# One decoder-layer step on one core: the front of an mLSTM + pooling + MoE kernel rearranged in six places

## The reference

```python
x1 = LN1(alpha*x + W_out [pool_group(x) | mlstm_group(x)])
x2 = LN2(alpha*x1 + MoE(x1))            # top 4 of 32 experts, clamped SwiGLU
y  = x2 + sigmoid(x2 W_pg) * (p W_ple)
```

```python
def mlstm_chunk(carry, inp):
    C, n, m = carry
    ...
    m_t = jnp.maximum(inter, jnp.max(logD, axis=-1))
    Dw = jnp.exp(logD - m_t[..., None]); sc = jnp.exp(inter - m_t)
    qk  = jnp.einsum('bhtk,bhsk->bhts', q, k) * Dw
    num = jnp.einsum('bhts,bhsv->bhtv', qk, v) + sc * (C q)
    den = jnp.sum(qk, axis=-1) + sc * (n q)
    ...
    C_new = decay * C + jnp.einsum('bhsv,bhsk->bhvk', v * wk, k)
    n_new = decay * n + jnp.einsum('bhs,bhsk->bhk', wk, k)
```

## Time and profile before

| | us |
|---|---|
| median of 3 runs (lowest, highest) | 1123.28 (1123.21, 1123.94) |
| span of the profiled execution, first to last instruction | 1122.0 |
| median of the runs less that span (the profiled execution has no other time of its own) | 1.3 |
| PE busy | 1102.2 (98%) |
| DVE / ACT / POOL busy | 410.8 / 165.4 / 78.3 |
| DMA moved | 440.45 MB, mean 393 GB/s |

### The profile page before, as it was taken

How to read it: one execution, slowest core, us unless ns; L and a number is a source line. 1 busy time by engine, 2 the same in 40 slices (tenths; PEclk the granted TensorE clock), 3 DMA queues, 4 the chain that set the end, 5 groups by cost and what they waited for, 6 DMA issues and landing times.

```text
span 1122.0 us, 14800 instructions
## 1 busy us (share of the span) xinstructions
PE 1102.2 (98%) x5706; PEld 428.6 (38%) x5706; DVE 410.8 (37%) x875; ACT 165.4 (15%) x310; POOL 78.3 (7%) x102
## 2 busy tenths in 40 slices
PE   8999999999999999999999999999999999999998
PEld 6788433333333333333333333333333333323344
DVE  1657583333333333333333333333333333222255
ACT  1423141001000100010001100010001000100033
POOL 0756610000000000000000000000000000000000
PEclk9999999999999999999999999999999999999999
...
GB/s 318 261 341 240 253 286 403 427 428 428 429 428 429 429 427 429 427 429 428 430 428 428 429 427 429 429 429 428 428 429 428 429 429 429 427 429 427 428 280 39
DMA packets 47699, 440.45 MB, mean 393 GB/s; under 512 B 10512, under 2 KB 11788, under 8 KB 22741
## 3 DMA queue, kind: packets, MB, share of 16 engines
...
q10 hardware_dynamic: 292, 0.56, 0.1%
...
## 4 chain that ended last, share of the span: by engine, by line
PE 87%; DMA 10%; DVE 2%; ACT 0%; issue 0%; SPq 0%; DVEq 0%; ACTq 0%
PE bank L883 36%; PE bank L925 18%; DMA ring<-in_w_mlp 9%; PE bank L822 7%; PE bank L510 6%; PE bank L844 5%; PE bank L1001 2%; PE bank L686 2%; PE bank L857 2%; PE bank L907 2%; PE bank L870 1%; PE bank L914 1%; PE bank L850 1%; DMA ring<-in_w_in 1%; PE bank L836 1%
## 5 line engine op out<-in xcount | busy, mean ns | idle before, releaser
L883 PE MATMUL bank<-ring,proj 128*64 128x512 f32 x2048 | 466.0, 597 | 4.7 <-DMA ring<-in_w_mlp 4.7
L1395 DVE SCALAR_TENSOR_TENSOR xT<-bank,proj,xT 128x512 f32<-128x512 f32 x128 | 90.2, 747 | 440.9 <-PE bank L844 439.5
L883 PEld LDWEIGHTS bank<-ring,proj 128*64 128x64 f32 x2048 | 135.3, 136 | 288.7 <-issue 246.9
L925 PE MATMUL bank<-ring,wpool 128*64 128x512 f32 x1024 | 225.1, 592 | 0.0
L925 PEld LDWEIGHTS bank<-ring,wpool 128*64 128x64 f32 x1024 | 71.2, 136 | 130.0 <-issue 129.2
L1744 ACT ACTIVATE proj<-proj 128x256 f32<-128x256 f32 x64 | 26.7, 417 | 546.7 <-DVE proj L1424 546.7
L822 PE MATMUL bank<-xreg,proj 128*64 128x512 f32 (+1 forms) x396 | 95.4, 599 | 0.1
L510 PE MATMUL bank<-xT,ring 128*128 128x264 f32 x320 | 76.3, 396 | 2.9 <-DVE proj L1058 2.4
L844 PE MATMUL bank<-mixT 64*128 64x512 f32 x264 | 74.5, 641 | 0.5 <-ACT mixT L1752 0.5
L510 PEld LDWEIGHTS bank<-xT,ring 128*128 128x128 f32 x320 | 61.4, 195 | 15.6 <-DVE proj L1058 2.8
L1752 ACT COPY mixT<-bank 128x512 f32<-128x512 f32 x32 | 18.8, 586 | 232.4 <-PE bank L925 232.4
...
## 6 DMA issues: line engine op xcount, KB each, us to landing
...
```

Of the source, the lines that this page charges most:

```text
L883: last = pe.matmul(bank[q][BLOCK * t:BLOCK * (t + 1), :], xgT[:, k % 4, k // 4, :], ring[:, s, col:col + 512], start=False, stop=(k == KD ...
L925: last = pe.matmul(bank[4][BLOCK * h:BLOCK * (h + 1), :], aT[:, m, BLOCK * t:BLOCK * (t + 1)], w[:, k % 2, 512 * h:512 * h + 512], start=F ...
L1395: ins = STT(total[:, c, s], ins_bank[h][:, :], gate_table[:, c, bass.ds(n, 1)], total[:, c, s], ALU.mult, ALU.add)
```

## The change

It has six parts. (1) `vtok`, `vweighted` and `CT` get a 129th column per head (`WIDE`), which is 1 in `vtok`; the six groups of one-column products per head (L535, L544, L663) go, and a product's result is 129 columns, heads 0 to 2 in one bank and head 3 in bank 3. (2) The maxima diagonal of chunk 1 stands on partitions 32 to 35 instead of 0 to 3. (3) DVE copies tile 4 out between the two chunks' rows instead of behind both. (4) The first 512 columns of `w_in` are loaded as two halves of 256 columns with all rows (1 KB runs instead of 2 KB), and the other constants are issued by SP between them instead of by ACT at the start. (5) POOL clears a tile `blank`, and PE multiplies it with itself four times, 256 columns each, before it waits for the identity. (6) The transpose of `scq` is moved ahead of the second `mix`.

```diff
-xreg = sb("xreg", [P, 3 * D])
-lnreg = sb("lnreg", [P, 2 * D])
+xreg = sb("xreg", [P, 3 * D + 8])
+lnreg = sb("lnreg", [P, 2 * D + 8])
+blank = mixT[:, :, :].rearrange("p k n -> p (k n)")[:, 1024:1024 + 2 * P]
...
+def wide(main, at, lo, hi):
+    if hi <= 3:
+        return main[:, 0:3 * WIDE].rearrange("p (h d) -> p h d", h=3)[:, lo:hi]
+    return bank[3][:, at:at + WIDE].unsqueeze(1)
+V0, M0, V1 = 0, WIDE, 2 * WIDE
+I1, M1 = V0, M0
+HEAD_SETS = ((0, 3), (3, 4))
...
-xtok = xreg[:, :].rearrange("p (c d) -> p c d", c=3)
+xtok = xreg[:, 0:3 * D].rearrange("p (c d) -> p c d", c=3)
-vtok = xreg[:, 1024:2048].rearrange("p (c h d) -> p c h d", c=2, h=HEADS)
-decayed = xreg[:, 2048:3072].rearrange("p (c h t) -> p c h t", c=2, h=HEADS)
+vtok = xreg[:, 1024:2056].rearrange("p (c h d) -> p c h d", c=2, h=HEADS)
+decayed = xreg[:, 2056:3080].rearrange("p (c h t) -> p c h t", c=2, h=HEADS)
-vweighted = lnreg[:, 1024:1536].rearrange("p (h d) -> p h d", h=HEADS)
-CT = lnreg[:, 1536:2048].rearrange("p (h d) -> p h d", h=HEADS)
+vweighted = lnreg[:, 1024:1540].rearrange("p (h d) -> p h d", h=HEADS)
+CT = lnreg[:, 1540:2056].rearrange("p (h d) -> p h d", h=HEADS)
...
-maxdiag = [xreg[0:HEADS, 2048 + 512 * c:2560 + 512 * c].rearrange("p (h t) -> p h t", h=HEADS)
+maxdiag = [xreg[32 * c:32 * c + HEADS, 2056 + 512 * c:2568 + 512 * c].rearrange("p (h t) -> p h t", h=HEADS)
...
-    for c, (t0, n) in enumerate(CHUNKS):
+    for c in (0, 1, 2):
+        t0, n = CHUNKS[c]
+    def load_columns(half):
+        sp.dma_start(ring[:, half, :].rearrange("p (k n) -> p k n", k=KD),
+                     w_in[0, :, 256 * half:256 * half + 256].rearrange("(k p) n -> p k n", p=P))\
+          .then_inc(sem(f"slot{half}"), 16)
...
-    load_block(0)
+    load_columns(0)
+    sp.dma_start(cst[:, C_ID + P:C_END], consts[:, C_ID + P:C_END]).then_inc(sem("cst_in"), 16)
+    load_columns(1)
...
+    pe.wait_ge(sem("pool_chain"), 2)
+    for _ in range(4):
+        pe.matmul(bank[7][:, 0:2 * P], blank[:, 0:P], blank, start=True, stop=True)
...
-            s = 2 * b + k // 4
-            if j == 0 and k % 4 == 0:
-                pe.wait_ge(sem(f"slot{s}"), 16)
-            w = ring[:, s, :].rearrange("p (k n) -> p k n", k=4)
-            last = pe.matmul(bank[t % 2][:, 0:TOK], w[:, k % 4, j * P:(j + 1) * P], xT[:, k, :],
-                             start=(k == 0), stop=(k == KD - 1))
+            if b == 0:
+                if j % 2 == 0 and k == 0:
+                    pe.wait_ge(sem(f"slot{j // 2}"), 16)
+                w = ring[:, j // 2, :].rearrange("p (k n) -> p k n", k=KD)[:, k, (j % 2) * P:(j % 2 + 1) * P]
+            else:
+                s = 2 * b + k // 4
+                if j == 0 and k % 4 == 0:
+                    pe.wait_ge(sem(f"slot{s}"), 16)
+                w = ring[:, s, :].rearrange("p (k n) -> p k n", k=4)[:, k % 4, j * P:(j + 1) * P]
+            last = pe.matmul(bank[t % 2][:, 0:TOK], w, xT[:, k, :], start=(k == 0), stop=(k == KD - 1))
...
         pe.matmul(bank[7][:, 0:TOK], wpool[:, g, :], proj[:, T_U + g, :], start=True, stop=True)\
           .then_inc(sem("pool_ps"), 1)
-    def values(c, dst, dden):
+    def values(c, dst, at):
         for h in range(HEADS):
-            pe.matmul(dst[:, h * P:(h + 1) * P], decayed[:, c, h, :], vtok[:, c, h, :], start=True, stop=True)
+            last = pe.matmul(wide(dst, at, *HEAD_SETS[h // 3])[:, h % 3, :], decayed[:, c, h, :], vtok[:, c, h, :],
+                             start=True, stop=True)
+        return last
+    def memory(c, dst, at):
         for h in range(HEADS):
-            last = pe.matmul(dden[:, h:h + 1], decayed[:, c, h, :], ones[:, 0:1], start=True, stop=True)
-        return last
-    def memory(c, dst, dn):
-        for h in range(HEADS):
-            pe.matmul(dst[:, h * P:(h + 1) * P], ktok[:, c, h, :], vweighted[:, h, :], start=True, stop=True)
-        for h in range(HEADS):
-            w0 = 4 * (ROW_WK + c) + h
-            last = pe.matmul(dn[:, h:h + 1], ktok[:, c, h, :], gcol[:, w0:w0 + 1], start=True, stop=True)
+            last = pe.matmul(wide(dst, at, *HEAD_SETS[h // 3])[:, h % 3, :], ktok[:, c, h, :], vweighted[:, h, :],
+                             start=True, stop=True)
         return last
     def turn_heads(c):
...
-    values(0, bank[2], bank[3][:, 0:4]).then_inc(sem("num_ps"), 1)
+    values(0, bank[2], V0).then_inc(sem("num_ps"), 1)
-    memory(0, bank[4], bank[3][:, 4:8]).then_inc(sem("mem_ps"), 1)
+    memory(0, bank[4], M0).then_inc(sem("mem_ps"), 1)
...
-    values(1, bank[5], bank[3][:, 8:12])
+    values(1, bank[5], V1)
-        pe.matmul(bank[2][:, h * P:(h + 1) * P], proj[:, T_Q + h, P:2 * P], CT[:, h, :], start=True, stop=True)
-    for h in range(HEADS):
-        last = pe.matmul(bank[3][:, 12 + h:13 + h], proj[:, T_Q + h, P:2 * P], nstate[:, h:h + 1],
+        last = pe.matmul(wide(bank[2], I1, *HEAD_SETS[h // 3])[:, h % 3, :], proj[:, T_Q + h, P:2 * P], CT[:, h, :],
-    memory(1, bank[4], bank[3][:, 16:20]).then_inc(sem("mem_ps"), 1)
+    memory(1, bank[4], M1).then_inc(sem("mem_ps"), 1)
...
     mix(0, first, range(4))
     pe.wait_ge(sem("sbc_done"), 2)
     turn_heads(0)
-    pe.wait_ge(sem("num_done"), 2)
-    mix(1, second, range(4))
     pe.wait_ge(sem("cfin_done"), 1)
     pe.wait_ge(sem("scq_ready"), 1)
     pe.transpose(bank[7][0:STATES, 0:P], scq, ident).then_inc(sem("scq_ps"), 1)
+    pe.wait_ge(sem("num_done"), 2)
+    mix(1, second, range(4))
     pe.wait_ge(sem("hT_done"), 1)
     mix(0, first, range(4, KD))
     turn_heads(1)
     pe.wait_ge(sem("ct_ready"), 2)
     for h in range(HEADS):
-        pe.transpose(bank[4][:, h * P:(h + 1) * P], CT[:, h, :], ident)
-    pe.transpose(bank[3][0:HEADS, 0:P], nstate, ident).then_inc(sem("cfin_ps"), 1)
+        pe.transpose(bank[4][:, h * P:(h + 1) * P], CT[:, h, 0:HD], ident)
+    pe.transpose(bank[3][0:HEADS, 0:P], CT[:, :, HD], ident).then_inc(sem("cfin_ps"), 1)
     pe.wait_ge(sem("sample_heads"), 2)
     pe.transpose(bank[7][:, P:P + STATES], srow[:, SY, :], ident[0:STATES, 0:STATES])\
...
-    empty_tile(4)
+        if c == 0:
+            empty_tile(4)
...
-    step(dve.tensor_copy(vtok[:, 0], bank[2][:, :].rearrange("p (h d) -> p h d", h=HEADS)))
+    more(dve.memset(vtok[:, :, :, HD:WIDE], 1.0))
+    step(dve.tensor_copy(vtok[:, 0, :, 0:HD], bank[2][:, :].rearrange("p (h d) -> p h d", h=HEADS)))
-            .to_broadcast([P, HEADS, P]), ALU.mult), "vw_ready")
+            .to_broadcast([P, HEADS, WIDE]), ALU.mult), "vw_ready")
-    step(dve.tensor_copy(nstate, bank[3][:, 4:8]))
-    step(dve.tensor_copy(den, bank[3][:, 0:4]))
-    step(dve.tensor_copy(CT, bank[4][:, :].rearrange("p (h d) -> p h d", h=HEADS)), "ct_ready")
-    step(dve.tensor_copy(hout[:, 0], bank[2][:, :].rearrange("p (h t) -> p h t", h=HEADS)), "num_done")
+    for lo, hi in HEAD_SETS:
+        more(dve.tensor_copy(CT[:, lo:hi, :], wide(bank[4], M0, lo, hi)))
+        more(dve.tensor_copy(hout[:, 0, lo:hi], wide(bank[2], V0, lo, hi)[:, :, 0:HD]))
+        more(dve.tensor_copy(den[:, lo:hi], wide(bank[2], V0, lo, hi)[:, :, HD]))
+    dve.wait_ge(sem("dve_chain"), counts["dve_chain"])
+    dve.engine_nop().then_inc(sem("num_done"), 1)
+    more(dve.engine_nop(), "ct_ready")
-            .to_broadcast([P, HEADS, P]), ALU.mult), "vw_ready")
+            .to_broadcast([P, HEADS, WIDE]), ALU.mult), "vw_ready")
...
-    step(TT(hout[:, 1], bank[2][:, :].rearrange("p (h t) -> p h t", h=HEADS),
-            sc1.unsqueeze(2).to_broadcast([P, HEADS, P]), ALU.mult))
-    step(TT(hout[:, 1], hout[:, 1], bank[5][:, :].rearrange("p (h t) -> p h t", h=HEADS), ALU.add))
-    step(TT(den, bank[3][:, 12:16], sc1, ALU.mult))
-    step(TT(den, den, bank[3][:, 8:12], ALU.add), "num_done")
+    for lo, hi in HEAD_SETS:
+        inter = wide(bank[2], I1, lo, hi)
+        more(TT(hout[:, 1, lo:hi], inter[:, :, 0:HD],
+                sc1[:, lo:hi].unsqueeze(2).to_broadcast([P, hi - lo, P]), ALU.mult))
+        more(TT(den[:, lo:hi], inter[:, :, HD], sc1[:, lo:hi], ALU.mult))
+    dve.wait_ge(sem("dve_chain"), counts["dve_chain"])
+    for lo, hi in HEAD_SETS:
+        inner = wide(bank[5], V1, lo, hi)
+        more(TT(hout[:, 1, lo:hi], hout[:, 1, lo:hi], inner[:, :, 0:HD], ALU.add))
+        more(TT(den[:, lo:hi], den[:, lo:hi], inner[:, :, HD], ALU.add))
+    dve.wait_ge(sem("dve_chain"), counts["dve_chain"])
+    dve.engine_nop().then_inc(sem("num_done"), 1)
-    step(TT(CT, CT, dec_b.unsqueeze(2).to_broadcast([P, HEADS, P]), ALU.mult))
-    step(TT(CT, CT, bank[4][:, :].rearrange("p (h d) -> p h d", h=HEADS), ALU.add))
-    step(TT(nstate, nstate, dec_b, ALU.mult))
-    step(TT(nstate, nstate, bank[3][:, 16:20], ALU.add), "ct_ready")
+    step(TT(CT, CT, dec_b.unsqueeze(2).to_broadcast([P, HEADS, WIDE]), ALU.mult))
+    for lo, hi in HEAD_SETS:
+        more(TT(CT[:, lo:hi, :], CT[:, lo:hi, :], wide(bank[4], M1, lo, hi), ALU.add))
+    dve.wait_ge(sem("dve_chain"), counts["dve_chain"])
```

(5 more changed lines are left out.)

4 lines of the change are left out of this document (2 added, 2 removed).

## The result

| | us |
|---|---|
| median of the changed kernel, 4 runs (lowest, highest) | 1113.53 (1113.17, 1115.05) |
| the kernel before on the same chip, 4 runs (lowest, highest) | 1123.61 (1123.21, 1124.52) |
| ratio | 0.9908, 95% interval 0.9896 to 0.9920 |
| profiled execution of the changed kernel: time, span | 1113.78, 1112.0 |

The change gains 10.1 us; the sum had 8.25. What happened is nearest to rival (B): PE asked for more than the forecast, and a new wait for DVE took a part of it back. In many executions, whichever the kernel, the granted clock falls for some 3.5 us somewhere in the front, which makes that execution 1.6 to 1.7 us longer (rows at the end); the two profiles compared here have no such stretch.

The account below looks back on a forecast made before the run. The weight stream was taken to bound the end, its start set by PE's way through the front. Gains 0.75 + 0.4 + 2.3 + 0.9 + 1.55 + 2.35 = 8.25 us gave 1115.0, from 1123.28; range 1113.3 to 1118.2.

Parts of the forecast that it names:

- rival (B): Front: clock stays high from the dummies on, q rows' chain makes PE wait for `vweighted`; gain 9.0 to 9.4, 1114.1; chance 0.10.
- first product: Front start: slot 0 lands near 9.2 and the first product starts at 9.6 instead of 10.36; gain 0.75, ends 0 and 1.0.
- What bounds the kernel: Expert loop: the weight stream sets the end, so PE reaching the loop X us earlier moves the end by X.
- (C): Loop start: early pair loads come too late, so the end does not follow; 3 to 4 us gained, 1119.5; chance 0.09.
- (D): Expert loop: tiles shifted by 32 and 64 bytes slow PE's operand reads; 4% gives 1126; chance 0.04.
- The clock behind the dummies: Tiles 0 and 1: dummies raise PE's clock, only partly held over turning x; gain 0.4 of at most 2.1.
- Column halves: First weight loads: 1 KB runs make 1 MB dearer by 0 to 0.9 us, taken as 0.25.
- The skill's rule: Turning of x: transposes do not engage the full clock, so the dummies' 0.4 would be 0 and the sum 0.4 smaller.
- Tile 4's copy: Before tile 6: PE's 2.36 us wait goes, 2.35, less 0.05 waiting for chunk 1's rows; gain 2.3.
- Row groups: Maxima products: row groups 0 and 32 run side by side, 1.8 us without drain halves; gain 0.9, ends 0 and 0.9.
- One-column products: Values groups: each removed group saves 0.79; first pair 1.55, other three 2.35, after small charges.
- The q rows: First pair of values groups: DVE's chain to `vweighted` lets L541 come forward 5.8 to 6.2; PE asks 5.15, so it fits.

Follow-up runs that it names:

- experiment 2: The changed kernel without the four dummy products: 1114.64 us, ratio 0.9897 to the kernel before.
- experiment 3: Kernel before with one part: dummies and blank tile alone, 1124.88 us, ratio 0.9997; constants alone on SP's queue behind slot 0, 1126.64 us, ratio 1.0012.

## Why the prediction was wrong, and where it was right

The gain up to the loop start, by stretches of PE's way, adds up to what was measured there (160.67 - 150.98):

| | forecast | measured |
|---|---|---|
| first product | 0.75 | 0.90 |
| tiles 0 and 1 run faster (the clock) | 0.4 | 2.07 |
| tile 4's copy, less the wait for the rows | 2.3 | 2.03 |
| maxima products | 0.9 | 0.88 |
| new wait before the first values product | 0 | -0.59 |
| one-column products | 3.9 | 4.40 |
| sum | 8.25 | 9.69 |

- **What bounds the kernel: right.** The front's gain went to the end, the late windows have the same 0.83 in 30, and (C) and (D) fell (L904 takes 597 ns, as L883 did).
- **The clock behind the dummies: the step that failed.** I took 0.4, a fifth of what could be had, and 2.07 came, which is the whole of it. The reason I gave was that "in the trace 5 us of the same turning did not bring the high level". I took that for a property of turning. In the runs it went with a turning that breaks off: unbroken, with nothing ahead, it did bring the high level (experiments 2 and 3). So the term had the cause wrong as well as the size: what set PE's clock free in the changed kernel can as well have been the constants' move, which lets the second token block come early enough for an unbroken turning, and the dummies would then not have been missed.
- **Column halves: put at nothing.** Beyond a price of 0.25 for their runs the sum had no term for them. But tile 0 of the kernel before needed both row halves, and its slow products hid the wait for the second. Alone, dummies or constants bring tile 1's end 0.57 forward and the time not at all (experiment 3); only with the column halves do the first product's 0.90 and the clock's 2.07 both count.
- **The skill's rule.** The rule of the Trainium skill (TensorE: Matmul & The Clock Gate, Part 4), that PE transposes do not engage the full clock, is not borne out here: 24 of them, with nothing ahead, were followed by products 0.22 apart. In the changed kernel the clock also outlasted 1.70 us of idle.
- **Tile 4's copy: gain right, next wait mis-sized.** 2.36 went; the wait for the rows was given as 0.05 and measured 0.54, most of it because L1126 took 0.35 for 0.22 and PE was through with tile 6 at 38.24, another 0.27 earlier than 43.84 - 2.97 - 2.36.
- **Row groups: right**, 0.88 for 0.9. TensorEngine Tiling (Array Packing) in the Trainium skill says that tiles operate independently; the run with one row group bears that out. No run put the two tiles in one bank.
- **One-column products: mis-sized**, 4.4 to 4.5 for 3.9, the rest being 0.1 in each following group.
- **The q rows: the number right, by another step of the chain.** The forecast said that L541 can come forward by 5.8 to 6.2, and it came forward by 6.02 (93.48 to 87.46). But it had `vweighted` hold it, and `vweighted` did not: it took 0.76 instead of 1.40 and was done in time. What PE waited for was `vtok`, before the first values product, which the forecast had not followed. That the number came out is in part luck. Both ways of loosening that chain take the wait away.
- **Rival (B)** came nearest, with 9.0 to 9.4 for the 9.69 at the loop start; the column terms make up the rest. The clock did stay high from the dummies on, but experiment 2 shows that it would have been high without them. Its new wait came at the place just named and was 0.59, not 1. At 0.10 its chance was too small: it rested on a guess about the clock where the trace gave only a bound.
